# Second layer's shared gate and up with the contraction outermost, each weight unit freed by its own quarter

## What is computed

```
def swiglu(t, wg, wu, wd):
    return (jax.nn.silu(t @ wg) * (t @ wu)) @ wd

def grouped_moe(h, router_w, router_bias, w_gate, w_up, w_down, sh_gate, sh_up, sh_down):
    ...
    out = swiglu(t, sh_gate, sh_up, sh_down)
    for e in range(N_EXPERTS):
        out = out + combine[:, e:e + 1] * swiglu(t, w_gate[e], w_up[e], w_down[e])
    return out.reshape(shp)
```

## Time and profile before

| what | us |
|---|---|
| median of 3 runs | 1641.71 |
| lowest, highest run | 1639.67, 1646.81 |
| the profiled execution, its time | 1640.55 |
| its span in the profile | 1638.4 |
| PE busy in it | 1445.5 |
| mean granted clock of PE | 0.952 |

### The profile page before, as it was taken

The page is one execution under the profiler, slowest core; times in us unless marked ns, Lnnn a source line. Parts: engine busy times, 40 slices in busy tenths (PEclk is TensorE's granted clock), DMA queues, the critical chain, the costliest instruction groups (busy, mean ns, idle before and its releaser), DMA issues.

```text
span 1638.4 us, 28948 instructions
## 1 busy us (share of the span) xinstructions
PE 1445.5 (88%) x12440; PEld 832.2 (51%) x12440; DVE 518.5 (32%) x918; ACT 378.3 (23%) x900; POOL 187.7 (11%) x207
## 2 busy tenths in 40 slices
PE   4799989899988999899999998996988999988766
PEld 2433445454544444365555555552845775554424
DVE  3255555544443221224121121132244331211103
ACT  2211334333424210130121121113053212211111
POOL 0000033223242200000011111000000000111100
PEclk9599989999989999979999999997999899999987
DMA  7355314344340442003999999990400349999992
GB/s 280 126 183 202 128 65 149 125 139 141 120 138 26 110 122 77 26 25 129 389 370 373 384 392 381 378 323 2 142 26 4 116 139 352 393 397 399 403 392 100
DMA packets 128132, 334.46 MB, mean 204 GB/s; under 512 B 13123, under 2 KB 60923, under 8 KB 121851
## 3 DMA queue, kind: packets, MB, share of 16 engines
q1 hardware_dynamic: 116027, 308.76, 51.8%
q0 software_dynamic: 6144, 12.60, 2.3%
q10 hardware_dynamic: 5824, 11.16, 1.9%
HBM read 325.65 MB, written 14.68 MB: 208 GB/s over the span
## 4 chain that ended last, share of the span: by engine, by line
PE 72%; SPq 9%; DMA 7%; DVE 5%; ACT 5%; issue 2%; DVEq 0%; ACTq 0%; POOLq 0%
PE ps L1379 12%; PE ps L1085 10%; PE ps L1102 7%; PE ps L1297 7%; SPq L517 6%; PE ps L1409 5%; PE ps L1333 4%; PE ps L1036 3%; PE ps L1423 3%; SPq L519 2%; PE ps L1190 2%; DMA ssb<-in_moe_w_up 2%; PE ps L1614 2%; PE ps L1526 2%; PE ps L1055 2%
## 5 line engine op out<-in xcount | busy, mean ns | idle before, releaser
L1379 PE MATMUL ps<-ring,ssb 128*32 128x256 f32 x2960 | 174.3, 383 | 14.4 <-DMA ring<-in_moe_w_up 12.0
L1085 PE MATMUL ps<-aT,ring 128*128 128x512 f32 x384 | 175.1, 605 | 0.0
L1379 PEld LDWEIGHTS ps<-ring,ssb 128*32 128x32 f32 x2960 | 106.0, 110 | 77.8 <-DMA ring<-in_moe_w_up 15.8
L2012 DVE COPY big<-ps 32x256 f32<-32x256 f32 x160 | 67.7, 423 | 180.8 <-PE ps L1409 179.1
L1085 PEld LDWEIGHTS ps<-aT,ring 128*128 128x128 f32 x384 | 71.6, 193 | 84.1 <-issue 84.0
L1102 PE MATMUL ps<-aT,ring 128*128 128x512 f32 x256 | 114.2, 595 | 0.0
L1297 PE MATMUL ps<-big,ring 128*128 128x512 f32 x256 | 110.2, 592 | 0.0
L2005 DVE TENSOR_TENSOR ssb<-ssb,ps 128x256 f32<-128x256 f32 (+3 forms) x32 | 15.6, 488 | 270.8 <-ACT ssb L907 270.8
L1409 PE MATMUL ps<-ring,ssb 128*32 128x256 f32 x1472 | 87.1, 389 | 13.6 <-ACT ssb L911 9.7
L816 ACT ACTIVATE ssb<-ps,ncum 128x128 f32<-128x128 f32 x256 | 73.3, 371 | 98.7 <-PE ps L1165 97.9
L916 ACT COPY big<-ps 32x256 f32<-32x256 f32 x160 | 58.0, 362 | 160.3 <-PE ps L1409 158.8
(11 more groups left out here) (288 smaller groups left out, 1854.0 us busy)
## 6 DMA issues: line engine op xcount, KB each, us to landing
ring<-in_ada_w SPq DMA_DIRECT2D x48, 1024.0 KB
ring<-in_moe_w_gate SPq DMA_DIRECT2D x75, 512.0 KB
ring<-in_moe_w_up SPq DMA_DIRECT2D x75, 512.0 KB
ring<-in_moe_w_down SPq DMA_DIRECT2D x37, 1024.0 KB
ring<-in_ssd_in_w SPq DMA_DIRECT2D x20, 1024.0 KB
tmp<-in_moe_w_down SPq DMA_DIRECT2D x14, 1024.0 KB
ssb<-in_moe_w_gate SPq DMA_DIRECT2D x27, 512.0 KB
ssb<-in_moe_w_up SPq DMA_DIRECT2D x27, 512.0 KB
```

Source lines behind the costliest of these rows:

```text
L1085: ins = pe.matmul(ps[:, bank, :], slot(u)[:, k, (i % 2) * P:(i % 2 + 1) * P], aT[:, k, :], start=(k == 0), stop=(k == KD - 1))
L1379: ins = pe.matmul(tiled_gu[32 * c:32 * c + 32, g, :].rearrange("p (r n) -> p r n", r=2), XgT[l][:, k * C + 32 * g:k * C + 32 * g + 32], pa ...
L2012: ins = dve.tensor_copy(Y[s % 2][32 * g:32 * g + 32, 256 * c:256 * c + 256], tiled_y[32 * c:32 * c + 32, g, :])
```

## The change

Layer 1's shared gate and up are computed in four quarters of the contraction rather than in four quarters of the columns. All eight results (four column blocks, gate and up) of 128 x 256 stay in PSUM at once: bank f holds gate in its first half and up in its second. Quarter j reads unit j alone, and the slot of unit j is freed at the end of quarter j (j = 0 to 2) or, as before, by the last count of `s_gu` (j = 3). In quarter 3 the blocks are finished one after another. The quarters stand on PE where the chunks stood. All silus of ACT and all products of DVE of layer 1's shared expert move behind `place` and `indices`, since no block is finished before the last quarter. The counts of `s_gu2[1]` that free the experts' units are three higher (`AHEAD_PIECES`). Layer 0 is as before.

```diff
         def unit_free(name, v):
 
             if name in ("sgu0", "sgu1"):
-                return s_gu[int(name[3])], KF
+                return (s_gu2[1], v + 1) if name == "sgu1" and v < 3 else (s_gu[int(name[3])], KF)
...
             if j < 4:
-                return s_gu2[l], 4 * s + j + 1
+                return s_gu2[l], AHEAD_PIECES[l] + 4 * s + j + 1
...
-                    act.activation(sg[f % 2][:, 0:n], ps[:, 2 * (f % 2), 0:n], ACT.Silu).then_inc(s_sg[l], 1)
+                    act.activation(sg[f % 2][:, 0:n], ps[:, f if l and not e else 2 * (f % 2), 0:n], ACT.Silu).then_inc(s_sg[l], 1)
...
-                chunk(0, 0)
+                if l == 0:
+                    chunk(0, 0)
...
-                for f in range(1, KF):
+                for f in range(1 - l, KF):
                     chunk(0, f)
...
+                def hidden_piece(j):
+
+                    arrived(pe, unit(0, j))
+                    w = pair_slot(unit(0, j))
+                    for f, k in [(f, k) for f in range(KF) for k in (2 * j, 2 * j + 1)] if j == 3 else \
+                            [(f, k) for k in (2 * j, 2 * j + 1) for f in range(KF)]:
+                        for r in range(2):
+                            ins = pe.matmul(ps[:, f, r * n:(r + 1) * n], w[:, k % 2, r, f * P:(f + 1) * P], aT[:, k, 0:n],
+                                            start=(k == 0 and r == 0), stop=(k == KD - 1), skip_group_check=True)
+                        if k == KD - 1:
+                            ins.then_inc(s_gu[l], 1)
+                    if j < 3:
+                        ins.then_inc(s_gu2[l], 1)
+
+                part = hidden_piece if l else lambda f: hidden_chunk(0, f)
...
-                chunk(0, 0)
-                chunk(0, 1)
-                place(l)
-                chunk(0, 2)
-                indices(l)
-                chunk(0, 3)
+                if l:
+                    place(l)
+                    indices(l)
+                    for f in range(KF):
+                        chunk(0, f)
```

More of the change, by code:

```diff
@@ L55 @@
 AHEAD_EXPERTS = [0, 1]
+AHEAD_PIECES = [0, 3]
 EMPTY = 8192
@@ L903, in tiled_act @@
                 G = step_rows(l, s) // 32
-                act.wait_ge(s_gu2[l], 4 * s + 4)
+                act.wait_ge(s_gu2[l], AHEAD_PIECES[l] + 4 * s + 4)
                 if s:
@@ L1436, in moe_pe @@
                 C = RANK_ROWS[l][0]
-                hidden_chunk(0, 0)
+                part(0)
                 for r in range(2 * nt):
@@ L1444, in moe_pe @@
                     ins.then_inc(s_mt8, 1)
-                hidden_chunk(0, 1)
+                part(1)
                 pe.wait_ge(s_sel, l + 1)
@@ L1455, in moe_pe @@
                 ins.then_inc(s_rk, 1)
-                hidden_chunk(0, 2)
+                part(2)
                 pe.wait_ge(s_oh, 4 * l + nt)
@@ L1464, in moe_pe @@
                 ins.then_inc(s_ix, 1)
-                hidden_chunk(0, 3)
+                part(3)
                 pe.wait_ge(s_mtv, 8 * l + 2 * nt)
@@ L2020, in chunk @@
                     dve.wait_ge(s_sg[l], KF * e + f + 1)
-                    dve.tensor_tensor((hidD if e else hid)[:, f, 0:n], sg[f % 2][:, 0:n], ps[:, 2 * (f % 2) + 1, 0:n], ALU.mult)\
-                        .then_inc(s_hid[l], 1)
+                    up = ps[:, f, n:2 * n] if l and not e else ps[:, 2 * (f % 2) + 1, 0:n]
+                    dve.tensor_tensor((hidD if e else hid)[:, f, 0:n], sg[f % 2][:, 0:n], up, ALU.mult).then_inc(s_hid[l], 1)
                 def outputs(e, w):
@@ L2038, in moe_dve @@
                     .then_inc(s_val, 1)
-                chunk(0, 0)
-                chunk(0, 1)
-                place(l)
-                chunk(0, 2)
-                indices(l)
-                chunk(0, 3)
+                if l:
[3 more added lines that the diff above has]
+                        chunk(0, f)
+                else:
+                    chunk(0, 0)
+                    chunk(0, 1)
+                    place(l)
+                    chunk(0, 2)
+                    indices(l)
+                    chunk(0, 3)
                 sparse = choose(dve, l)
```

## The result

| | before | changed |
|---|---|---|
| median of 20 runs each, us | 1645.27 | 1648.17 |
| the profiled execution: time, span | 1640.55, 1638.4 | 1650.92, 1649.1 |

The ratio is 1.0023, 95% interval 1.0012 to 1.0034: 3.8 us slower, between 2.0 and 5.6 (the two medians of the table lie 2.9 us apart), which is under the half per cent that was set as the bound of "no change". (The median of before over 20 runs lies 3.6 us above that of its first three.) The two profiled executions lie 10.4 us apart in time; of that 4.8 us had come before anything the change touches: the first shared matmul of layer 1 starts at 1303.46 in the one and at 1308.27 in the other.

A forecast was written before the change was run, and what follows sets the result against it. Bound by DMA from 1372 to 1604, its start set by the chain through the first gather and PE. 1640.55 + 5.4 (gather) + 0.3 (clock) = 1646.25 us, forecast 1647.4 against the three-run median; range 1640.5 to 1652.

The forecast's parts named there:

- What sets the end: Layer 1's mixture: the end hangs on the chain indices, first gather, PE, slots, DMA; step 1's four units are not on it.
- All of it counts: Unbroken DMA stretch after 1372: it starts later by PE's whole delay, nothing absorbs it, so the end moves as much.
- PE's matmuls at 0: Layer 1's shared gate and up: 16 matmuls of the same shapes in four places before and after, so 0 us.
- fewer waits at 0: PE's shared quarters: one unit rather than four awaited before the first, none for hidden; nothing was waited for, 0 us.
- SP's loads 4.8 us earlier, gain 0: Step 1's loads: first issue at 1332.6 instead of 1337.42; the burst ends before the gap of 1362 anyway, gain 0.
- The first gather, 9.0 us: Layer 1's first gather meets the moved loads: 9.0 us (5.8 to 10.5) instead of 3.26, PE's transposes 5.4 us later.
- DVE, 0.3 us: Between flag and `indices`: one product less on DVE, so the gather is issued 0.3 us earlier, at 1335.1.
- PE's clock, +0.3: PE after its longer pause before step 0: the transposes (1.10 us) also run at half clock, +0.3 us.
- The last rival: Step 0: gather takes 10.5 us and half clock lasts longer on gate and up; slower by over 0.5%, 1651.9; chance 0.16.
- the free gather: Layer 1's first gather slips through in about 3.3 us as before; only DVE's 0.3 stays, 1641.4 us; chance 0.17.
- the stream's start: Rival: the high-traffic DMA stretch begins 4.8 us earlier and ends as much earlier, 1636.9 us; chance 0.05.
- the slower case: Rival slower by over 0.5%: 10.5 us gather (+6.9) and longer half clock on step 0's gate and up, 1651.9; chance 0.16.

The follow-up runs named there:

- traffic_3: Kernel before plus three 1 MB DRAM-to-DRAM copies issued by SP right behind layer 1's flag; ratio to before 1.0049.
- late_release: Changed kernel with the early freeing undone: all four shared units of layer 1 freed by the last count of `s_gu`; ratio to before 0.9986.
- loads_after_gather: Changed kernel, units freed early, but SP's loads of step 1 wait until the first gather has landed; ratio to before 0.9998.
- burst_later: Two runs of the kernel before with SP's loads of step 1 held until PE's first transposes or first quarter of step 0; ratios 1.0008 and 1.0026.
- one_early: Changed kernel with only the unit of quarter 0 freed early, the other three by the last count; ratio to before 0.9984.
- burst_later_7: Kernel before with SP's loads of step 1 held until PE's first quarter of step 0's gate and up; ratio to before 1.0026.
- traffic_6: Kernel before plus six 1 MB DRAM-to-DRAM copies issued by SP behind layer 1's flag, ahead of step 1's loads; ratio to before 1.0067.
- before_again: Kernel before, unchanged, profiled a second time; shared down at 300.52 us from layer 1's first shared matmul, against 300.85; no ratio.
- after_again: Changed kernel, unaltered, profiled a second time; shared down at 307.05 us from layer 1's first shared matmul, against 306.65; no ratio.
- one_early_gidx: Changed kernel with only quarter 0's unit freed early and POOL's first gathers waiting for `gidx` alone, `sidx` before the first scatter; ratio to before 1.0004.
- late_release_gidx: Changed kernel with early freeing undone and POOL's first gathers waiting for `gidx` alone, `sidx` before the first scatter; ratio to before 0.9987.

## Why the prediction was right

The forecast was 1647.4 us and the median is 1648.17. That these lie 0.8 us apart is luck: the forecast stood on a median of three runs, 1641.71, and over 20 runs the kernel before has 1645.27. What was forecast of the change itself is slower by 5.7 us. The profiles say 5.8 to 6.5 and the ratio 3.8 (2.0 to 5.6), so the size was met on the profiled stretch, and for whole executions it was forecast half as large again as measured. The mechanism was the one that was forecast. Point by point:

- *What sets the end* was right: indices, gather 0, PE, slots, DMA. A delay of 6.0 to 6.3 us at the first down came out as 5.8 to 6.5 at the shared down (before and changed, two profiles each), and traffic_3 passed 7.0 to 7.3 on as 6.9 to 7.2. "All of it counts" holds for delays. It does not hold for gains: of about 2 us at the first down, late_release kept 0.3 to 0.6, after half clock in the down, and loads_after_gather, without it, 1.1 to 1.5.
- *PE's matmuls at 0* and *fewer waits at 0*: right, quarters two to four last 7.07, 7.15 and 7.15 us as the chunks did, and late_release has all of this without a loss.
- *SP's loads 4.8 us earlier, gain 0*: they are 4.6 to 4.9 earlier. The holds of burst_later show that a later start is mostly absorbed, and one_early that one unit loaded 5.0 us earlier than in late_release has its shared down only 0.25 us earlier. That three units earlier gain nothing by themselves was not run apart from the gather; the idle DMA engines at 1354 to 1358 speak for it. What is absorbed was nearly twice the 3.4 us that the expectation of burst_later_7 gave it.
- *The first gather, 9.0 us*: measured 7.8 and 8.2, so PE's transposes were 4.1 to 4.6 us later rather than 5.4. This was the term on which the forecast rested. Of the two ways to read its nearest rows, the 7.5 of the steady stream came closer than the 10.5 of a queue in order of issue, and traffic_6 spoke against such a queue. Weighing the two 10.5s so much was the mis-sizing: the third gather of layer 1, the nearest in kind, took 8.7 us in before_again and 8.8 in late_release, so its 10.5 was one high value. The Trainium skill's rule that the prediction cites (DMA: Bandwidth & Descriptors, Queues, rings and completion order) was on the side that the traces bear out.
- *DVE, 0.3 us*: the gather is issued at 32.02 in the mean of the six profiles with the order of before and at 31.78 in the mean of the six with the new order and the old index wait, 0.24 us earlier. The pause of PE that it shortened may have mattered more than the 0.3 itself (last section); that was not tested by itself.
- *PE's clock, +0.3*: measured 1.7 to 1.9. The transposes were at half clock (1.97 against 1.09, +0.88), as forecast but dearer: by the prediction's own price of 0.5 us for each us at half clock, 1.10 us of work there costs 1.1, not 0.3. And the 64 instructions behind them took 6.38 (6.14 in after_again) against 5.35, +0.8 to +1.0. This term was too small by 1.4 to 1.6 us and made good the 0.8 to 1.3 us that the gather had too many. The last rival's mechanism, longer half clock, was at work: some 10 us, from 1346 to 1356, rather than 3.3. PE stood for 2.7 us of that, so it cost less than the 3.3 us more that the rival put on it.
- *The rivals*: the free gather happens with one unit ahead but not with three; the stream's start is excluded; of the slower case the long half clock came true, but the gather stayed under 10.5 and the whole under half a per cent.

On the profiles the sum was right to 1 us with two terms off in opposite directions; that is luck in the last digit, not in the sign.

## What to carry to other kernels

Before a load is released earlier, ask what else will be on the DMA queues in that moment: a small transfer on the chain (here the first gather) went from 3.3 us to 7.4 behind 2 MB of loads and to 8 behind 3 MB, and lost nothing behind 1 MB that was through in time. Loads that feed a stage whose slots PE frees gained nothing here from an earlier start; the idle stretch of the DMA engines only moved. And a stretch of a long kernel is best compared from its own first instruction: in two pairs of profiles that repeated to 0.4 us, where whole executions scatter by 10.

## What was not expected of the hardware

- **Half clock and small differences of a pause.** PE's wait for the first gather was 1.53 to 1.64 us in five profiles (before, before_again, both burst_later, one_early_gidx); each shows half clock on gate and up of step 0 and a first down at 55.64 to 55.92. It was 0 to 1.3 us in four (late_release, one_early, loads_after_gather, late_release_gidx); none has half clock there, and the first down is at 52.93 to 53.91. So 0.3 to 0.5 us less of a wait went with some 2 us less at the first down (1.7 to 2.4). In late_release half clock came some 17 us later, behind the pauses around the product's transposes. Nine profiles are too few to call it a rule, and no run tried the pause by itself.
- **A gather's landing is a step in the traffic ahead of it**: 3.2 us with one unit issued 2.5 us before it, 4.9 with one issued 1.25 us before, 7.4 with two, 7.8 and 8.2 with three, 9.8 with three DRAM-to-DRAM copies and 10.6 with six.
